# Attention in units of two score maps, with a shorter hand-written order of its engines

## The reference, cut to what matters

```
# differential heads (4), each with two maps of 64 channels
s = einsum(q, k) * scale            # 512 queries x 768 keys (latent and context), per map
p = softmax(s);  a = p[map 0] - lam * p[map 1]
o = rms_norm(a @ v) * subln_g * (1 - lam_init)
# near heads (8), 64 channels
s_loc = einsum(q, k_neighbours) * scale + bias
s_ctx = einsum(q, k_ctx) * scale
o = softmax(concat[s_loc, s_ctx]) @ [v_neighbours, v_ctx]
out = concat[o_diff, o_near] @ w_out
```

## Time and profile before

| | us |
|---|---|
| median of 3 runs (4101.5 to 4109.29) | 4106.7 |
| the profiled execution, its own time | 4106.57 |
| its span in the trace | 4104.8 |
| attention, differential units (360.0 to 464.25) | 104.25 |
| attention, near units, to the first matmul of the projection (464.25 to 608.65) | 144.4 |

### The profile page before, as it was taken

The page is one execution under the profiler, slowest core; times in us unless marked ns, Lnnn a source line. Parts: engine busy times, 40 slices in busy tenths (PEclk is TensorE's granted clock), DMA queues, the critical chain, the costliest instruction groups (busy, mean ns, idle before and its releaser), DMA issues.

```text
span 4104.8 us, 48578 instructions
## 1 busy us (share of the span) xinstructions
PE 3913.2 (95%) x19304; PEld 3113.2 (76%) x19304; DVE 2505.0 (61%) x4442; ACT 1257.5 (31%) x1573; POOL 468.1 (11%) x222
## 2 busy tenths in 40 slices
PE   2998898999999998999999898999999989999998
PEld 2555566888888887888888677888888878888886
DVE  5654871495599974555555241892899945555555
ACT  1002443333355541111111233333455531111112
POOL 0000003444200000000000254444000000000000
PEclk9998899999999999999999899999999999999999
DMA  6562012144455555766665121344455556666663
GB/s 214 192 221 79 11 50 95 50 151 141 157 193 177 198 208 183 268 196 196 191 194 177 37 87 61 111 144 147 168 189 198 194 178 204 191 197 194 188 197 118
DMA packets 321589, 651.18 MB, mean 159 GB/s; under 512 B 18642, under 2 KB 151379, under 8 KB 300628
## 3 DMA queue, kind: packets, MB, share of 16 engines
q1 hardware_dynamic: 321364, 648.08, 48.2%
HBM read 511.69 MB, written 136.31 MB: 158 GB/s over the span
## 4 chain that ended last, share of the span: by engine, by line
PE 89%; DVE 7%; ACT 2%; issue 1%; DMA 1%; SPq 0%; DVEq 0%; ACTq 0%
PE ps L1090 34%; PE ps L1052 32%; PE ps L896 5%; PE ps L971 4%; PE ps L1023 4%; PE ps L1065 4%; PE ps L923 1%; DVE Ahot L1504 1%; PE ps L866 1%; PE ps L937 1%; PE ps L1007 1%; DVE macc L1215 1%; PE ps L955 1%; DVE xm L1189 1%; PE ps L853 0%
## 5 line engine op out<-in xcount | busy, mean ns | idle before, releaser
L1090 PE MATMUL ps<-Hhi,Vhi 128*128 128x512 f32 x2048 | 799.4, 390 | 20.8 <-DVE Hlo L1548 20.8
L1052 PE MATMUL ps<-xhi,Uhi 128*128 128x512 f32 x2048 | 811.0, 396 | 0.0
L1052 PE MATMUL ps<-xhi,Ulo 128*128 128x512 f32 x2048 | 799.0, 390 | 0.0
L1090 PE MATMUL ps<-Hlo,Vhi 128*128 128x512 f32 x2048 | 798.9, 390 | 0.0
L1090 PE MATMUL ps<-Hhi,Vlo 128*128 128x512 f32 x2048 | 798.6, 390 | 0.0
L1052 PE MATMUL ps<-xlo,Uhi 128*128 128x512 f32 x2048 | 796.7, 389 | 0.0
L1531 DVE TENSOR_TENSOR Vlo<-Vraw,Vhi 128x1024 fp32r<-128x1024 f32 x256 | 313.6, 1225 | 617.9 <-ACT Vhi L795 617.9
L795 ACT CAST Vhi<-Vraw 128x1024 fp32r<-128x1024 f32 x256 | 268.3, 1048 | 1123.9 <-PE ps L1090 1102.1
L1090 PEld LDWEIGHTS ps<-Hhi,Vhi 128*128 128x128 f32 x2048 | 385.7, 188 | 101.9 <-issue 21.6
L1052 PEld LDWEIGHTS ps<-xhi,Ulo 128*128 128x128 f32 x2048 | 384.3, 188 | 82.9
L1090 PEld LDWEIGHTS ps<-Hhi,Vlo 128*128 128x128 f32 x2048 | 385.8, 188 | 80.4
(11 more groups left out here) (216 smaller groups left out, 4209.7 us busy)
## 6 DMA issues: line engine op xcount, KB each, us to landing
Uraw<-in_UT SPq DMA_DIRECT2D x128, 1024.0 KB, 5.5
Vraw<-in_V SPq DMA_DIRECT2D x256, 512.0 KB, 3.6
act_scratch<-act_st SPq DMA_DIRECT2D x256, 256.0 KB, 5.2
G_scratch<-G_st SPq DMA_DIRECT2D x32, 2048.0 KB, 8.7
act<-act_scratch SPq DMA_DIRECT2D x256, 256.0 KB, 3.5
Gin<-G_scratch SPq DMA_DIRECT2D x64, 1024.0 KB, 7.0
modw<-in_w_mod SPq DMA_DIRECT2D x48, 1024.0 KB, 5.1
ring<-in_query SPq DMA_DIRECT2D x8, 2048.0 KB, 8.0
```

The source lines that it names most:

```text
L1052: mm = nc.tensor.matmul(up_bank(m), w, x[:, k, :], start=(k == 0 and j == 0), stop=(k == KT - 1 and j == 2))
L1090: mm = nc.tensor.matmul(down_bank(d), w[m % 3][:, cols], x[m % 3][:, :], start=(m == 0 and j == 0), stop=(m == NT - 1 and j == 2))
```

## The change

- Units are 32: the 16 differential ones, and 16 near ones that hold two heads each (partitions 0 to 63 and 64 to 127). Every unit has two maps, in three PSUM banks; two sets of three alternate by unit. The middle bank is shared by both maps, so S(u) runs in four parts with a wait (`bank_shared`) before the last, and its columns are cut 512, 256, 512, 256.
- M(u): one maximum over both maps for differential units. For near units the maximum of the context part first, and then for each map one `tensor_tensor_reduce` that adds the bias in PSUM and takes the maximum. The bias table of two heads is scaled and masked in one instruction. `Sbuf` is gone.
- T(u) goes through one bank (6) in pieces of four blocks: two pieces for differential units, three for near ones. Each piece waits until ACT has copied the one before it.
- AV(u) of a near unit writes two heads to the two halves of the partitions. ACT, no longer DVE, copies the output, and for differential units squares it; PE sums the squares of 128 columns (`square_sum`) in the next step but one; DVE collects them in `oms` (`mean_squares`).
- The root is taken once, for all heads, in step 19. DVE's inversions and products (`normed`) lie in steps 21, 23, 25 and 27.
- The rows of `oT` are rounded and split as they become ready, in the order `K_ORDER`; one remains for the end. The projection takes its rows in that order.
- SP's load of query chunk 2 moves behind the wait for the first projection row; two bias tables of two heads each are in other places.

The core of the diff:

```diff
-            for u in range(len(units) + 2):
-                if u + 1 < len(units):
+            for u in range(NU + 1):
+                if 2 <= u and u - 2 < HEAD_END:
+                    square_sum(u - 2)
+                if u + 1 < NU:
                     scores(u + 1)
-                if 1 <= u <= len(units):
-                    pe.wait_ge(probs_ready, u)
-
-                    at_least(pe, probsT_ready, u - 1)
-                    for kt in range(KK):
-                        mm = nc.tensor.transpose(wide(2)[:, kt * P:(kt + 1) * P],
-                                                 Abuf[:, (u - 1) % 2, kt * P:(kt + 1) * P], ident[:, :])
-                    mm.then_inc(probsT_mm, 1)
-                if u >= 2:
-                    av(u - 2)
+                if u < NU:
+                    turn(u, 0)
+                if u >= 1:
+                    av(u - 1)
+                if u < NU:
+                    for n in range(1, len(pieces(u))):
+                        turn(u, n)
...
+                at_least(pe, exp_done, 2 * (u - 1))
+                q, kx = (qaT, kaT) if kind == "diff" else (qbT, kbT)
+                for m, c0, c1 in ((0, 0, T), (1, 0, TC), (1, TC, TK), (0, T, TK)):
+                    lo = DH * m
+                    if (m, c1) == (0, TK):
+
+                        pe.wait_ge(bank_shared, u + 1)
+                    mm = nc.tensor.matmul(scores_of(u)[:, m, c0:c1], q[lo:lo + DH, h, qt * P:(qt + 1) * P],
+                                          kx[lo:lo + DH, h, c0:c1], start=True, stop=True)
+                    if (m, c0) == (1, 0):
+                        mm.then_inc(bank_shared, 1)
+                mm.then_inc(score_mm, 1)
...
+            def turn(u, n):
+                b0, b1 = pieces(u)[n]
+                pe.wait_ge(probs_ready, u + 1)
+
+                at_least(pe, probsT_ready, turned_before(u) + n)
+                for b in range(b0, b1):
+                    mm = nc.tensor.transpose(turned[:, (b - b0) * P:(b - b0 + 1) * P],
+                                             Abuf[u % 2][:, b * P:(b + 1) * P], ident[:, :])
+                mm.then_inc(probsT_mm, 1)
...
+            def square_sum(u):
+                pe.wait_ge(osq_ready, u + 1)
+                nc.tensor.matmul(osum_bank, ones[:, :], osq[:, u % 2, :], start=True, stop=True).then_inc(osum_mm, 1)
...
+                if kind == "diff":
+                    step(nc.vector.tensor_reduce(mx[:, j:j + 2], scores_of(u), AX, ALU.max))
+                else:
+                    step(nc.vector.tensor_reduce(mxc[:, u % 2, :], scores_of(u)[:, :, T:TK], AX, ALU.max))
                     row = NA_ROWS - 1 - 2 * qt
+                    for m in range(2):
+                        near = scores_of(u)[:, m, 0:T]
+                        last = nc.vector.tensor_tensor_reduce(
+                            out=near, in0=near,
+                            in1=btab[h % 2][:, m, row:row + NA_ROWS, :].rearrange("p r c -> p (r c)"),
+                            scale=1.0, scalar=mxc[:, u % 2, m:m + 1], op0=ALU.add, op1=ALU.max,
+                            accum_out=mx[:, j + m:j + m + 1])
...
+            exps(0, 0)
+            exps(0, 1)
+            for u in range(NU + 1):
+                for n in range(2):
+                    if u + 1 < NU:
+                        exps(u + 1, n)
+                    if u < NU:
+                        probsT_out(u, n)
+                if u >= 1:
+                    outputs(u - 1)
+                if u < NU and maps(u) == 2:
+                    probsT_out(u, 2)
+                if u == HEAD_END + 3:
+                    act_e.wait_ge(oms_ready, HEAD_END)
+                    nc.scalar.activation(oms[:, :, :], oms[:, :, :], ACT.Sqrt).then_inc(orms_ready, 1)
...
+            for u in range(NU):
+                if u + 1 < NU:
+                    maxima(u + 1)
+                if 2 <= u and u - 2 < HEAD_END:
+                    mean_squares(u - 2)
+                probabilities(u)
+                if u in NORM_AT:
+                    normed(NORM_AT[u])
+                for _ in range(SPLIT_AT.get(u - 1, 0)):
+                    rest_of_rows(done_rows)
+                    done_rows += 1
```

More of the change, by code:

```diff
@@ L385, in backbone, with maps, pieces, turned_before @@
                 units.append(("diff", h, qt))
-        for h in range(HB):
+        for h in range(HB // 2):
             for qt in range(TT):
                 units.append(("near", h, qt))
[L389 to L393, removed]
-        HEAD_END = HA * TT
+        NU = len(units)
+        HEAD_END = HA * TT
+        K_ORDER = [HA, 0, 1, HA + 1, 2, 3, HA + 2, HA + 3]
+        SPLIT_AT = {22: 2, 24: 1, 26: 2, 28: 1, 30: 1}
+        NORM_AT = {21: 0, 23: 1, 25: 2, 27: 3}
+        def maps(u):
+            return 1 if units[u][0] == "diff" else 2
+        def pieces(u):
+            return ((0, 4), (4, KK)) if maps(u) == 1 else ((0, 4), (4, 8), (8, 2 * KK))
+        def turned_before(u):
+            return sum(len(pieces(w)) for w in range(max(u, 0)))
         sh1, sc1, g1, sh2, sc2, g2 = [KT * n for n in range(6)]
@@ L686, in _ @@
[L686 to L697, removed]
-                if u >= 2:
-                    finish(u - 2)
@@ L700, in _, with exps @@
[L700 to L707, removed]
+            def exps(u, m):
+                j = 2 * u + m
+                if m == 0:
+                    act_e.wait_ge(nmax_ready, u + 1)
+                    at_least(act_e, probs_ready, u - 1)
+                nc.scalar.activation(Ebuf[:, j % 4, :], scores_of(u)[:, m, :], ACT.Exp, bias=nmx[:, j:j + 1],
+                                     scale=QK_SCALE, accum_out=zs[:, j:j + 1]).then_inc(exp_done, 1)
@@ L960, in _ @@
-            pe.wait_ge(o_out, len(units))
-            pe.wait_ge(o_normed, HA)
+                if u < NU:
[5 more added lines that the diff above has]
+                        turn(u, n)
+            pe.wait_ge(o_out, NU)
+            pe.wait_ge(oms_ready, HEAD_END)
             def mix_products(g, ready, count, tile, sem, bias=None):
@@ L1257, in _ @@
             step(nc.vector.tensor_scalar(lamv[:, 5:6], lamv[:, 4:5], -LAM_INIT, None, ALU.add))
+            step(nc.vector.tensor_scalar(mask[:, :], mask[:, :], 1.0 / QK_SCALE, None, ALU.mult))
             def maxima(u):
                 kind, h, qt = units[u]
[L1262 to L1276, removed]
[L1277 to L1289 removed]
@@ new lines, in maxima @@
+                j = 2 * u
+                if kind == "near" and qt == 0:
+                    dve.wait_ge(bias_in[h % 2], 16 * (h // 2 + 1))
+                    table = btab[h % 2][:, :, :, :].rearrange("p h s k -> p (h s) k")
+                    step(nc.vector.scalar_tensor_tensor(out=table, in0=table, scalar=1.0 / QK_SCALE,
+                                                        in1=mask[:, :].unsqueeze(1).to_broadcast([P, 32, GRID_W]),
+                                                        op0=ALU.mult, op1=ALU.add))
@@ L1335, in _ @@
-            maxima(0)
-            for u in range(len(units)):
-                if u + 1 < len(units):
-                    maxima(u + 1)
-                probabilities(u)
-                if u >= 2:
-                    outputs(u - 2)
-            outputs(len(units) - 2)
-            outputs(len(units) - 1)
-            for k in range(KT):
-                dve.wait_ge(o_hi, k + 1)
+                j = 2 * u
+                dve.wait_ge(exp_done, j + 2)
+                step(nc.vector.reciprocal(rz[:, j:j + 2], zs[:, j:j + 2]))
@@ new lines, in probabilities @@
+                at_least(dve, probsT_mm, turned_before(u - 1))
+                if kind == "diff":
+                    to = Abuf[u % 2][:, 0:TK]
+                    step(nc.vector.tensor_tensor(nlr[:, u:u + 1], rz[:, j + 1:j + 2], lamv[:, 5:6], ALU.mult))
+                    step(nc.vector.tensor_scalar(to, Ebuf[:, (j + 1) % 4, :], nlr[:, u:u + 1], None, ALU.mult))
+                    last = nc.vector.scalar_tensor_tensor(out=to, in0=Ebuf[:, j % 4, :], scalar=rz[:, j:j + 1],
+                                                          in1=to, op0=ALU.mult, op1=ALU.add)
+                else:
+                    for m in range(2):
+                        last = nc.vector.tensor_scalar(Abuf[u % 2][:, m * TK:(m + 1) * TK], Ebuf[:, (j + m) % 4, :],
+                                                       rz[:, j + m:j + m + 1], None, ALU.mult)
```

174 lines of the change are left out of this document (81 added, 93 removed).

## The result

The changed kernel takes 4266.87 us, median of four runs (4261.12 to 4272.09), against 4105.84 before: a ratio of 1.0392, 95% interval 1.0374 to 1.0410. That is 161 us more. The direction was forecast; 4204 and the range up to 4250 were too low.

The account below looks back on a forecast made before the run. Attention would be bound by a closed wait between DVE and PE, each unit costing its sum: 172.6 us differential plus 174 near, together 346 against 248.65, 97 more, so 4204 us from 4106.57; range 4150 to 4250.

Parts of the forecast that it names:

- the ring: Each unit: M(u+1), Pr(u), T(u), rest of PE's step, S(u+2), M(u+2) in sequence; unit time is their sum.
- The rival of the busiest engine: Attention stage: DVE's work sets the pace, 158 us of stage, 91 less, 4016 us in all; chance 0.06.
- DVE's 4.05 us a unit: Differential unit: DVE's own work, 4.28 us less 0.17 for one long maximum and some 0.06 for one product.
- The sums for either clock: Unit times at full and half clock: differential 9.4 and 12.7 us, near 10.0 and 14.3 us.
- AV of a near pair: Near unit: 24 products on two array halves, taken as 2.2 us, between 1.5 side by side and 3.0 in sequence.
- S of two maps: Scores of one unit on PE: 1.57 us at full clock, twice that at half clock.
- The drain: End of the near part: the last unit's drain takes about as long as a unit.
- From M(0) to M(1): Start of the differential part: about 4.6 us between the first two maxima, as before the change.
- The step that failed is the clock's share: Attention stage: half clock for 0.55 of the differential part and 0.2 of the near part.
- the 174 of the forecast: Near part: 16 units at 10.0 + 0.2 x 4.3 = 10.9 us, 174 us in all.
- The rival "half clock throughout": Attention stage at half clock: 195 us differential and 229 near, 175 more, 4281 us; chance 0.10.
- the signs named in the prediction: Differential units 9 to 12 us, near 9.5 to 11; DVE idle some 5, PE some 4; clock near 0.7.

Follow-up runs that it names:

- opened in the new kernel: Changed kernel with S(u+2) issued ahead of T(u) on TensorE, everything else the same: 4065.8 us.
- closed in the old one: Kernel before the change with only TensorE's order altered: T(u) and AV(u-1) in step u, a head's norm sum behind the next scores: 4378.69 us.
- kernels with scores ahead: Changed kernel with S(u+2) issued ahead of T(u), 4065.8 us, and versions adding later sums of squares, later remainders or reordered S parts, down to 4043.2 us.
- the last one: Changed kernel with S(u+2) ahead of T(u), square_sum behind those scores, remainders one step later and the shared bank's part of S first: 4043.2 us.
- the kernel with eight useless products: Changed kernel with eight extra products of ones and the identity on TensorE behind S(u+1) in each unit, results overwritten: 4188.97 us.

## Why the prediction was right and wrong

**The mechanism was right.** Closing the ring makes the loss, by the test from both sides: opened in the new kernel, 201 us less; closed in the old one, 273 us more. The rival of the busiest engine falls for this order. The kernels with scores ahead come nearer to it, 184.6 us of stage in the last one against the 158 worked out, but DVE's 4.05 us a unit are not reached: PE's list (4.51) and then the loop through exp (4.33) stand before it. Those kernels also show that the change's other parts, with an order that keeps the unit of slack, bring 40 to 63 us.

**The sums for either clock were about right.** Differential 9.4 and 12.7 against 9.55 and 13.23; near 10.0 and 14.3 against 9.68 and 13.65, the latter with the clock up in the pause and at the very end of the work. Of single terms:

- AV of a near pair at the full clock is 1.53 us for 24 products, as 12 products on one half do. I took 2.2. The Trainium skill, TensorEngine Tiling (Array Packing), Key Properties, says that different tiles can load weights and multiply in parallel. The trace agrees for halves by columns, with this 1.53. Timeline of PE at the end of the kernel after:

```profile
767.18 1.53 PE L992 MATMUL ps<-ATbuf,vb 128*64 128x128 f32 x24 [0.68 <-ACT ATbuf L708]
```

- S of two maps costs 1.89, not 1.57, through the wait for the shared bank. It takes back half of the 0.67 that AV came under its price; the 0.35 left are about what 9.68 lies under 10.0.
- The drain is 20.7 us (748.34, the last unit's first maximum, to 769.08), 7 us more than the length of a unit, which I had put down for it.
- From M(0) to M(1) it takes 1.9 us, not 4.6, since M(1) now follows M(0) directly.
- The square needed no table of its own; no load stands in the timeline above. SP's moved load cost nothing that shows: outside the stage the two spans differ by 2.5 us.

**The step that failed is the clock's share.** It read: "I take half clock for 0.55 of the differential part [...] In a near unit the pause is 3.6 and the unbroken work 6 us; I take 0.2." A granted clock of 0.66 and 0.63 is half clock for 2 x (1 - 0.66) = 0.68 and 0.74 of the time. And the share of the time is still too low for the near part: the sum multiplies it by the price of PE's work at half clock, and the quarter of the time with the clock up lay in the pause, where it buys nothing. With 13.65 for a unit the factor in 10.0 + 0.2 x 4.3 should have been 0.85. With unit costs of 13.7 in place of 10.9, the near part alone is 16 x 2.8 = 45 us longer; with the drain's 7 this makes the 52 by which 225.5 exceeds the 174 of the forecast. The differential part adds 11 (183.6 for 172.6): its 15 units took 12.1 on average, not 11.2, less what M(0) to M(1) saved. Sum 63: 4204 + 63 = 4267, and the 2.5 us outside the stage make up the 4269.59 of the profiled execution.

The reasoning behind it looked at pause and work as two chances of about equal weight. In the earlier trace rows the clock fell with a pause, and came back only when PE had been at work again for a good while. I gave the near unit's 6 us of work the power to lift the clock in time. The clock does rise in each unit, but when the work is nearly over; the high clock is then spent on DVE's pause. Nor was that work unbroken: PE waits 0.77 us for ACT's copy before the last transposes (648.65); the sum has 0.585 for this copy, and the 6 us run across it. The rival "half clock throughout", with a chance of 0.10 and 4281, was the one that came nearest, 14 us above the measured time. The Trainium skill, TensorE: Matmul & The Clock Gate, HAM oscillation, tells of a kernel whose bursts of matmuls start slow each time after a wait. The trace agrees in both parts: every unit's first four transposes take 1.1 us, where they take 0.66 at the full clock in the kernel with eight useless products. It was wrong of me to let it count for the differential part alone.

Of the signs named in the prediction most came: PE did wait for Pr, for 4.2 us, and `square_sum` for ACT's square, 0.8; AV of 24 products came out near 1.5, and the clock at 0.66 and 0.63. DVE did wait for scores, but in the unit shown for 9.1 us where I had named 5. Differential units of 9 to 12 came in 7 of 15, the others took 13.2. The near units at 9.5 to 11 failed.

## What to carry to other kernels

Write each engine's list of one loop step side by side and follow the way around through all of them. Here the scores of u+2 stood in PE's list behind the transposes of u, these need DVE's Pr(u), and Pr(u) stands in DVE's list behind the maximum of u+1, which needs the scores of u+1. If there is such a way around, the step costs the sum of all engines on it and not the longest, however little each has to do.

Then ask what the pause does to TensorE's clock. In this kernel a pause of 3.8 to 4.2 us in each step kept PE's work at half clock in the near units and in 8 of 15 differential ones, although PE's work between two pauses took 9 to 10 us, with one gap of 0.8 in it. Where a trace shows that pauses of such a length bring the clock down, reckon first with half clock for all of TensorE's work in the ring.

Larger units are a gain of their own, and no cure for the order: here the new form of the work gained in both orders, by 40 and 112 us, and closing the ring cost 201 and 273. Keep one unit in flight between the engines.

## What the runs showed of the hardware

- Useless products can pay: 496 matmul instructions of PE in pauses made the closed-ring kernel 78 us faster (4188.97 for 4266.87), and with half as many the gain of 2 us is within the scatter.
- The fused pass (add a table, take the maximum, write PSUM) takes 757 ns for 512 columns with an accumulator read of 142 ns behind it that overlaps the next pass; plain L1278, which writes SBUF, took 691 for as many columns.
- A maximum over two maps in one instruction returns both in 1.757 us, 0.145 less than two of 0.951.
- The four parts of S, 512 and 256 columns on each half of the rows, run side by side in both orders, but the wait for the shared bank can open a gap: S takes 1.56 us where the part that is waited for comes first, and 1.89 where it comes second, with 0.46 us of idle time in the weight loads before the last part.
- The granted clock can be high for a quarter of the time and help nothing: in the near units of the kernel after it was 0.90 over PE's pause of 3.76 us and 0.50 to 0.56 over its work.
